# A gate's sigmoid taken as a tanh, and inverse roots taken as powers on GpSimd, in a hybrid attention, S5 and PEER layer step

## The reference, cut to what matters

```
q = partial_rope(rms_norm(q, q_norm_g), pos)      # norms over the 64 dims of each of 16 heads
k = partial_rope(rms_norm(k, k_norm_g), pos)
o = diff_attn(...)                                # softmax(a) - lam * softmax(b), times v
o = rms_norm(o, subln_g) * (1.0 - lam_init)       # over the 128 dims of each of 8 heads
y = gelu(ssm(...))
y = y * sigmoid(y @ w_glu + b_glu)                # the gate
x = x + concat(o, y) @ w_out
x = x + peer_ffn(rms_norm(x, norm2_g), ...)       # experts: most of the time, not touched
rms_norm(x, g) = x * rsqrt(mean(x * x) + 1e-6) * g
```

## Time and profile before

| | |
|---|---|
| runs, us | 2263.26, 2268.69, 2263.33 (median 2263.33) |
| profiled execution, span | 2270.2 us (no time apart from the span is given) |
| TensorE busy | 2182.4 us (96%) |
| VectorE busy | 1711.6 us (75%) |
| ScalarE busy | 1120.6 us (49%) |
| GpSimd busy | 591.4 us (26%) |
| granted TensorE clock, mean | 0.988 |
| chain that ended last | TensorE 54%, issue 20%, GpSimd 12%, VectorE 11%, ScalarE 2% |

### The profile page before, as it was taken

One profiled execution on the slowest core, in us unless ns is written; L12 is line 12 of the kernel. 1 busy time (PEld: TensorE's weight loads), 2 busy tenths in 40 slices (PEclk: granted clock), 3 DMA queues, 4 the chain that ended last, 5 costly groups with the idle time before them and its releaser, 6 DMA issues.

```text
span 2270.2 us, 34759 instructions
## 1 busy us (share of the span) xinstructions
PE 2182.4 (96%) x12720; PEld 1907.4 (84%) x12720; DVE 1711.6 (75%) x2968; ACT 1120.6 (49%) x2099; POOL 591.4 (26%) x445
## 2 busy tenths in 40 slices
PE   7899899899999989999999999999999999999998
PEld 7786687778899989999888888888888888888887
DVE  8957884665466981888388888877778898878866
ACT  4233445654544534554455554555555554555554
POOL 4002330000176898548311111111101111111100
PEclk9899999999999999999999999999999999999999
DMA  6542236223443445676888997888779988787964
GB/s 228 127 119 76 75 98 226 95 87 118 154 169 142 158 149 186 214 226 230 279 326 347 376 359 297 327 318 327 285 285 359 358 349 333 306 335 302 350 218 162
DMA packets 126534, 537.55 MB, mean 237 GB/s; under 512 B 27648, under 2 KB 61872, under 8 KB 65680
## 3 DMA queue, kind: packets, MB, share of 16 engines
q1 hardware_dynamic: 61888, 358.62, 44.2%
q0 software_dynamic: 19888, 139.85, 14.9%
q10 hardware_dynamic: 44640, 37.56, 5.4%
HBM read 507.02 MB, written 28.38 MB: 236 GB/s over the span
## 4 chain that ended last, share of the span: by engine, by line
PE 54%; issue 20%; POOL 12%; DVE 11%; ACT 2%; ACTq 0%; DMA 0%; POOLq 0%; DVEq 0%
POOL w_parts L505 12%; PE psum L1968 10%; PE psum L1989 10%; PE psum L1990 10%; PE psum L1991 10%; PE psum L1969 5%; DVE experts L936 5%; DVE w_parts L936 3%; PE psum L1617 1%; DVE experts L1526 1%; PE psum L1619 1%; PE psum L1618 1%; ACT w_parts L534 1%; DVE experts L1521 1%; PE psum L1600 1%
## 5 line engine op out<-in xcount | busy, mean ns | idle before, releaser
L534 ACT ACTIVATE w_parts<-ring 128x512 fp32r<-128x512 f32 x1296 | 807.6, 630 | 822.2 <-PE psum L1991 339.4
L936 DVE TENSOR_TENSOR w_parts<-ring,w_parts 128x512 fp32r<-128x512 f32 x1040 | 703.1, 693 | 389.1 <-ACT w_parts L534 383.7
L1968 PE MATMUL psum<-x_parts,w_parts 128*128 128x512 f32 x1280 | 453.0, 399 | 3.1 <-DVE w_parts L936 1.2
L1593 PE MATMUL psum<-x_parts,w_parts 128*128 128x256 f32 (+1 forms) x1344 | 412.0, 307 | 25.2 <-POOL w_parts L505 13.8
L505 POOL TENSOR_TENSOR w_parts<-ring,w_parts 128x512 fp32r<-128x512 f32 x256 | 361.3, 1423 | 196.8 <-ACT w_parts L534 191.2
L1989 PE MATMUL psum<-w_parts,h_parts 128*128 128x512 f32 x1024 | 398.9, 390 | 4.6 <-DVE h_parts L936 2.7
L1991 PE MATMUL psum<-w_parts,h_parts 128*128 128x512 f32 x1024 | 398.4, 389 | 0.0
L1990 PE MATMUL psum<-w_parts,h_parts 128*128 128x512 f32 x1024 | 398.4, 389 | 0.0
L1594 PE MATMUL psum<-x_parts,w_parts 128*128 128x256 f32 (+1 forms) x1344 | 397.4, 296 | 0.0
L1595 PE MATMUL psum<-x_parts,w_parts 128*128 128x256 f32 (+1 forms) x1344 | 397.2, 296 | 0.0
L1969 PE MATMUL psum<-x_parts,w_parts 128*128 128x256 f32 x1280 | 358.7, 280 | 0.0
(11 more groups left out here) (237 smaller groups left out, 2549.1 us busy)
## 6 DMA issues: line engine op xcount, KB each, us to landing
ring<-in_peer_u SPq DMA_DIRECT2D x128, 1024.0 KB, 4.8
ring<-in_peer_v SPq DMA_DIRECT2D x128, 1024.0 KB, 5.1
ring<-in_w_in SPq DMA_DIRECT2D x32, 1024.0 KB, 4.9
ring<-in_w_out SPq DMA_DIRECT2D x16, 1024.0 KB, 4.8
ring<-in_w_pq SPq DMA_DIRECT2D x16, 1024.0 KB, 4.8
g_tmp<-experts ACTq DMA_DIRECT2D x16, 1024.0 KB, 5.9
experts<-g_tmp ACTq DMA_DIRECT2D x16, 1024.0 KB, 8.1
experts<-in_xT SPq DMA_DIRECT2D x8, 640.0 KB, 9.0
```

The lines of the kernel that those rows point to most:

```text
L534: act.activation(w_parts[:, q, 0, :], ring[:, b % SLOTS, 512 * q:512 * (q + 1)], ACT.Copy).then_inc(S["w_hi"], 1)
L936: return dve.tensor_tensor(out, a, b, op)
L1593: pe.matmul(out, w_parts[:, q, 0, c], moving(0), start=start, stop=False)
L1968: pe.matmul(bank(b % 2), w_parts[:, q, 0, 128 * d:128 * d + 128], both_of(dc), start=dc == 0, stop=False)
```

## The change

The head norms' squares are scaled by 1/8 ahead of squaring, so their sum is already the mean; VectorE adds epsilon alone. ScalarE's square root and VectorE's reciprocal, in the head norms and in the output norms, are one tensor_tensor with the operation pow on GpSimd, with a tile of -0.5 as second operand. GpSimd's queue gets m = 0 ahead of turn x = 2, m = 1 and 2 ahead of x = 3, m = 3 ahead of x = 7, m = 4 and 5 behind the turns, and the three output tiles behind the loads of the S5 outputs. Sigmoid(z) is taken as (tanh(z/2) + 1)/2: ScalarE's function is Tanh with scale 0.5, VectorE's bias is halved once (one more instruction at p = 20), the 1 is added in `gated`, and the half is put into `s_high` and `s_low`.

```diff
+            pool.memset(power, -0.5).then_inc(S["power"], 1)
+            def head_factors(m):
+                r = TILES[m % NT][1]
+                pool.wait_ge(S["hvar"], m + 1)
+                pool.tensor_tensor(hr[0:r, :], hv[0:r, :], power[0:r, :], ALU.pow).then_inc(S["hstd"], 1)
+            def output_factors(n):
+                r = TILES[n][1]
+                pool.wait_ge(S["ovar"], n + 1)
+                pool.tensor_tensor(orr[0:r, :], ov[0:r, :], power[0:r, 0:HEADS], ALU.pow).then_inc(S["ostd"], 1)
...
+            pool.wait_ge(S["power"], 1)
             for x in range(8):
                 rr, ri, cre, cim, ncim = ca_parts(x)
+                for m in ((), (), (0,), (1, 2), (), (), (), (3,))[x]:
+                    head_factors(m)
                 if x >= 2:
                     pool.wait_ge(S["y_mm"], x - 1)
...
+            head_factors(4)
+            head_factors(5)
             pool.wait_ge(S["ca"], 8)
...
+            for n in range(NT):
+                output_factors(n)
             pool.wait_ge(S["o_ok"], NT)
...
-                act.activation(sq_head[0:r, :], (q_tok, k_tok)[kind][0:r, n, :], ACT.Square).then_inc(S["qsq"], 1)
-            def head_std(m):
-                r = TILES[m % NT][1]
-                act.wait_ge(S["hvar"], m + 1)
-                act.activation(hv[0:r, :], hv[0:r, :], ACT.Sqrt).then_inc(S["hstd"], 1)
+                act.activation(sq_head[0:r, :], (q_tok, k_tok)[kind][0:r, n, :], ACT.Square, scale=HD ** -0.5).then_inc(S["qsq"], 1)
...
-            def output_std(n):
-                r = TILES[n][1]
-                act.wait_ge(S["ovar"], n + 1)
-                act.activation(ov[0:r, :], ov[0:r, :], ACT.Sqrt).then_inc(S["ostd"], 1)
...
+                if k == 0:
+                    act.wait_ge(S["b_half"], 1)
-                act.activation(zb[k % 3], bank((k + 2) % 4, T), ACT.Sigmoid, bias=b_glu[:, k:k + 1]).then_inc(S["glu_s"], 1)
+                act.activation(zb[k % 3], bank((k + 2) % 4, T), ACT.Tanh, bias=b_glu[:, k:k + 1], scale=0.5).then_inc(S["glu_s"], 1)
...
-                act.activation(in_time(x_parts[:, 0, 8 + k, :]), by_step(zb[k % 3]), ACT.Copy).then_inc(S["s_hi"], 1)
+                act.activation(in_time(x_parts[:, 0, 8 + k, :]), by_step(zb[k % 3]), ACT.Copy, scale=0.5).then_inc(S["s_hi"], 1)
...
+                dve.tensor_scalar(b_glu, b_glu, 0.5, None, ALU.mult).then_inc(S["b_half"], 1)
...
-                var_of(hv[0:r, :], hs[0:r, :], HD).then_inc(S["hvar"], 1)
+                dve.tensor_scalar(hv[0:r, :], hs[0:r, :], EPS, None, ALU.add).then_inc(S["hvar"], 1)
...
-                chain(dve.reciprocal(hr[0:r, :], hv[0:r, :]))
...
-                chain(dve.reciprocal(orr[0:r, :], ov[0:r, :]))
...
-                tt(zb[k % 3], zb[k % 3], yT[:, k, :], ALU.mult).then_inc(S["s_ok"], 1)
+                dve.scalar_tensor_tensor(zb[k % 3], zb[k % 3], 1.0, yT[:, k, :], ALU.add, ALU.mult).then_inc(S["s_ok"], 1)
...
-                tt(in_time(x_parts[:, 1, 8 + k, :]), by_step(zb[k % 3]), in_time(x_parts[:, 0, 8 + k, :].bitcast(F32)), ALU.subtract).then_inc(S["s_lo"], 1)
+                dve.scalar_tensor_tensor(in_time(x_parts[:, 1, 8 + k, :]), by_step(zb[k % 3]), 0.5, in_time(x_parts[:, 0, 8 + k, :].bitcast(F32)),
+                                         ALU.mult, ALU.subtract).then_inc(S["s_lo"], 1)
```

More of the change, by code:

```diff
@@ L147, in build @@
         os_, ov, orr = stat(HEADS), stat(HEADS), stat(HEADS)
+        power = stat(16)
         mx, nb, z, rz = stat(3, 2), stat(3, 2), stat(3, 2), stat(3, 2)
@@ L250, in bank @@
             return psum[:, b, 0:n]
-        names = """consts g1 x0 x1 x2 x3 x_hi1 x_lo1 sq1 ones ss1 rb rbs rbt rtr rst s5in
+        names = """consts b_half power g1 x0 x1 x2 x3 x_hi1 x_lo1 sq1 ones ss1 rb rbs rbt rtr rst s5in
             slot0 slot1 slot2 slot3 w_hi f_lo w_lo v_lo w_used
@@ L736, in _ @@
                         squares(kind, n)
-                    if 0 <= n < NT and late == 2:
-                        head_std(NT * kind + n)
                 for f in range(6):
@@ L755, in _ @@
                         exponentials(u)
-                for n in range(NT):
-                    if p == O_NORM[n] + 2 - (n == 2):
-                        output_std(n)
                 for m in range(2 * NT):
```

## The result

The changed kernel takes 2274.68 us (median of 5 runs, 2269.76 to 2277.33) against 2267.39 us for the kernel before (5 runs, 2263.26 to 2268.69). The ratio is 1.0031, with an interval of 1.0016 to 1.0045: **slower, by about 7.0 us (3.6 to 10.2)**. The time lies in the forecast's range, but on the side to which it gave a chance of 0.25.

The account below looks back on a forecast made before the run. TensorE's waits were the bound: on ScalarE's sigmoids in attention, on VectorE in the head norms. Terms -4.2 + 2.5 + 1.6, with half a slow stretch about -2 us, gave 2261.3 us from the median; range 2254 to 2282.

Parts of the forecast that it names:

- w: Duration of one power on GpSimd, taken as 1.4 us, with 0.2 to 6 us kept in the range.
- rival 1: Head norms, tiles m = 1, 2, 4, 5: VectorE stands behind GpSimd; +6 us at w = 3; chance 0.25.
- the forecast's case: Whole kernel: 2261.3 us, own range 2257 to 2268, chance 0.50.
- (a): First gates: the table load ahead of the sigmoids goes, gain 1.3 us.
- (b): Second gates: table loads around root, exponentials and sigmoids go, gain 1.3 us at the end of the group.
- (c): Output tile 1: two table loads around the root go, gain 1.1 us of TensorE's wait for VectorE.
- (d): Table load ahead of the last GELU copies goes, gain 0.5 us.
- (f): Slow clock after the wait at 449.00: may go, 2.4 us per 5 us stretch; up to 5 us in the range.
- The place at m = 1: Head norms: the power stands behind turn x = 2, making VectorE 1.2 us late at the end, plus w.
- Rival 2: Faster: a short power in the head norms (w = 0.5) and no slow clock stretch, 2255.8 us; chance 0.17.
- Rival 3: Gates: Tanh does not use Exp's table, so four loads stay, about 2264.8 us; chance 0.05.
- Rival 4: ScalarE: a table switch costs more than its load, so removed loads give more, about 2256 us; chance 0.03.

Follow-up runs that it names:

- the other execution of before: The kernel before, unchanged, profiled once more: 2266.89 us, span 2264.8.
- both parts alone: Two kernels, each against the kernel before: only the tanh gate with scaled squares, 0.9998 twice; only the output norms' powers on GpSimd, 0.9992 twice.

## Why the prediction was wrong

**The step that failed is the size of w.** "I take w = 1.4 us: if a power needs some thirty steps per element" had no row behind it; measured are 2.91 to 3.26 us for 128x16 and 3.88 for 64x16. The mechanism, the place and the line by which the loss grows with w were those of rival 1, "VectorE stands behind GpSimd", which gave +6 at w = 3 and passed 0.3% from 3.1 on. It came in at about 3.2 and +7.0. By its own formula with the measured durations q loses 0.9 + 2.91 + (3.88 - 1.2) = 6.5; measured 6.8. k would lose 3.2 + 0.2 + (3.88 - 1.2) = 6.1; measured up to the last wait 6.2, or 7.5 against the other execution of before. That the whole came out so near the rival's number is in part luck: with 4.2 us of gain 12.6 would make +8.4, but the attention gave 7.0 to 8.2 and not 4.2, and the clock moved the rest. Two sums of the rivals were off, without weight: by the formula as written, k at w = 3 is 5.0 and not 4.7 (10.7 in all, which is what the limit of 3.1 goes by; at w = 6 it is 22.7 and not 24), and at w = 0.5 it is 0.7 and not 0.3. The bounds of 0.2 and 6.95 us were right, and between them the nearest rows were of products, which said nothing on a power. With a price so open, the 0.50 for the forecast's case was too much.

**Point by point.** The loads: 16 gone, one come, as said. (a) and (b): the gates' waits fell by 2.1 us together where I counted 2.6; the wait of 2.33 became 1.30, as "down to about 1" had it. (c): the 1.10 is gone. (d): nothing, though the load is gone. Behind the last GELU ScalarE's queue issues eight DMAs (L619, L602 before), and the next copies wait for these; the issue took 5.75 us before (348.13 to 353.88) and now this, in ScalarE's timeline:

```profile
355.20 7.04 ACTq L619 DMA_DIRECT2D y_tmp<-experts  x8
```

So the 1.28 us of the load went into a longer issue. The other profiles agree: 7.0 us with the product and with powers twice, where the load is gone too, and 5.6 with the head roots on ScalarE, where it stands. Why the issue is longer wasn't looked into. The waits of the stretch fell from 13.8 to 11.2, 2.6 us in all. (f), which I left out of the sum, came: the busy time of C to D fell by 5.6 us for the same work, at a clock of 0.98 against 0.95. It isn't sure: with powers twice or ahead of the turns, and in both parts alone, the clock there is 0.95 or 0.96 and less of it comes. The place at m = 1: VectorE idle for 8.03 us where I had about 5; 1.5 of the 3 us more are the power's, the rest is the turn's, which ended later after the sum than I had worked out. The products there took 3.42 against 3.4 forecast. Output powers: 2.0 and 1.6 us, no one waits for them, as said. The median used as a base, 2263.33, was of three runs; 5 to 35 runs of the same kernel gave 2267.4 to 2268.3, so 4 us of the forecast's number was the base.

**The other rivals.** Rival 2 wanted a short power, and the product in its place shows it: 0.2 to 1.2 us in place of the power gives 0.9976, 5.4 us faster than before; the prediction had 7.5. Rival 3 falls: there is one load for all of the exponentials and tanhs together. The set table of the Trainium skill (ScalarE: Activation LUTs, the section on table sets) said so, and the trace agrees. Rival 4 falls too. The load at 376.21 and the exponential behind it, from ScalarE's timeline of the changed kernel:

```profile
376.21 1.28 ACT L643 ACT_TABLE_LOAD   x1
377.53 0.37 ACT L643 ACTIVATE experts<-psum,small 128x128 f32<-128x128 f32 x1
```

0.04 us lie between them, and 0.02 us between the instruction ahead (375.74, 0.45 long) and the load. The drain of 1380 ns for each switch, stated by the Trainium skill (ScalarE: Activation LUTs, What ACT_TABLE_LOAD costs), isn't seen in this trace; by an estimate from it the exponential would have started at about 378.9.

## What to carry to other kernels

Before an operation is moved to an idle engine, measure it alone in the size in which it will be used, on that engine: an estimate by "steps" was out by more than two here, and the sign of the whole change hung on it. What matters for a factor is how long after its sum the consumer wants it: the output norms had microseconds to spare and their powers were free, the head norms had some 1 to 4 us, and all but the first paid. A loss in one stretch is best read between waits of the same kind, since the clock behind them moves a stretch by a few us in either direction. A change of several parts is best kept by parts; here the version with the tanh and the output powers, and the head roots left where they were, is the one to keep.

## What the runs showed of the hardware that was not expected

- GpSimd's power costs about 0.167 us for each column and 0.35 us besides, from 8 to 48 columns, whatever the number of rows (2.89, 2.90 and 2.91 us for 32, 64 and 128 rows of 16 columns).
- Two-operand work of VectorE and GpSimd slows each other in both directions: the six products at m = 1 take 3.42 us alone and 6.08 beside a turn; the turn's 128x512 product takes 1.10 or 1.11 us alone and up to 2.13 beside them (276.06, turn x = 3 of the changed kernel, beside the products of m = 2). So a wait for the other engine's turn is not all lost, since the work behind it runs alone and faster: with a product for the power a wait of 5.34 us cost 1.8 us at piece 90.
- On GpSimd the first instruction of 64x16 numbers after the wait for its sum took about 1 us more, whatever it did: a power 3.88 against 2.90, a product 1.20 against 0.21.
- The same kernel's time up to A was 247.8 us in one execution and 243.8 in another, with clocks of 0.95 and 0.98 ahead of all that the change touches. Differences of a few us between two spans say nothing about an edit.
